# K/V preparation of the even layers, moved into the rest of their input projection

## The reference, cut to what matters

```python
def even_mixer(h, hc, w_in, ...):                 # w_in: 2048 x 5632
    k, v, q, bu, bv, ga, gb = split(h @ w_in, [512, 512, 1536, 512, 512, 1536, 512])
    q = apply_rope(rms_norm(heads(q, 12), q_g), cos, sin)
    k = apply_rope(rms_norm(heads(k, 4), k_g), cos, sin)    # per head of 128, then rotary
    attn = softmax(q k^T / sqrt(128)) v                     # 3 q heads share one k/v head
    sgu  = chunk_mlp(bu, bv, ...)
    out  = concat[attn * silu(ga), sgu * silu(gb)] @ w_out
```

## Time and profile before

| | us |
|---|---|
| median of 6 runs | 13523.53 |
| lowest, highest | 13475.0, 13628.33 |
| the profiled execution | 13583.81 |
| its span (core 1, the slowest) | 13582.2 |
| fastest core's span in it (core 4) | 13418.8 |

### The profile page before, as it was taken

How to read it: one execution, slowest core, us unless ns; L and a number is a source line. 1 busy time by engine, 2 the same in 40 slices (tenths; PEclk the granted TensorE clock), 3 DMA queues, 4 the chain that set the end, 5 groups by cost and what they waited for, 6 DMA issues and landing times.

```text
span 13582.2 us, 135689 instructions; the slowest of 8 cores (13418.8 to 13582.2 us)
## 1 busy us (share of the span) xinstructions
PE 6333.6 (47%) x36080; PEld 3450.9 (25%) x36080; DVE 4255.2 (31%) x6204; ACT 3173.7 (23%) x5611; POOL 2232.9 (16%) x1638
## 2 busy tenths in 40 slices
PE   2299155567691221021558953555849411211137
PEld 2144033343240111010223422333424211110014
DVE  0200432321212666416221023322121156652441
ACT  0200055530100222224111003555020012222330
POOL 0000322210002222222100022222000032223220
PEclk9599577777795555565667866777869755555558
DMA  7543110158432000111763321011953200002123
GB/s 113 184 108 107 59 34 30 37 93 188 120 90 60 11 11 11 56 52 40 132 181 103 100 67 40 32 34 35 186 161 93 87 9 11 11 13 85 38 55 102
DMA packets 649348, 1011.42 MB, mean 74 GB/s; under 512 B 112476, under 2 KB 523924, under 8 KB 590740
## 3 DMA queue, kind: packets, MB, share of 16 engines
q1 hardware_dynamic: 313144, 782.53, 17.3%
q0 software_dynamic: 335456, 220.22, 12.4%
HBM read 922.94 MB, written 299.89 MB: 90 GB/s over the span
## 4 chain that ended last, share of the span: by engine, by line
PE 40%; DVE 22%; DMA 12%; issue 10%; POOL 8%; ACT 7%; DVEq 1%; another core or an unknown queue 0%; POOLq 0%; SPq 0%; ACTq 0%
DVE PB L1104 3%; DMA ZY<-X 3%; PE gps_279 L433 1%; DVE lxc L1262 1%; PE gps_280 L433 1%; PE gps_282 L433 1%; PE gps_281 L433 1%; PE gps_48 L433 1%; PE gps_49 L433 1%; DMA adaw_18<-ada_w 1%; PE gps_50 L433 1%; PE gps_51 L433 1%; POOL htn L457 1%; DVE PB L1102 1%; POOL htb L466 1%
## 5 line engine op out<-in xcount | busy, mean ns | idle before, releaser
L1104 DVE TENSOR_TENSOR PB<-PB,X 128x576 f32<-128x576 f32 x224 | 425.2, 1898 | 23.0 <-DVE PB L1102 1.4
L593 ACT ACT_TABLE_LOAD x34 | 43.6, 1283 | 935.4 <-PE epS_313 L591 256.0
L451 POOL TENSOR_SCALAR hss<-hss 128x4 f32<-128x4 f32 (+1 forms) x72 | 14.3, 198 | 1161.5 <-DVE hss L449 1161.5
L1262 DVE SCALAR_TENSOR_TENSOR lxc<-lxd,lcw,lxc 128x255 f32<-128x255 f32 (+2 forms) x96 | 199.8, 2081 | 10.4 <-DVE lxc L1259 0.5
L572 PE MATMUL epT_311<-identb,rot 128*128 128x128 bf16 x144 | 21.1, 301 | 374.1 <-DVE rot L470 369.6
L572 PE MATMUL epT_80<-identb,rot 128*128 128x128 bf16 x144 | 21.1, 302 | 373.5 <-DVE rot L470 369.0
L649 PE MATMUL epG<-vnb,WST 128*128 128x128 bf16 x144 | 21.1, 301 | 360.4 <-POOL vnb L646 360.4
L1275 PE MATMUL lps_468<-lxcb,lwa_459 128*128 128x512 bf16 (+1 forms) x16 | 7.6, 478 | 372.2 <-ACT lxcb L1265 364.4
L1275 PE MATMUL lps_237<-lxcb,lwa_228 128*128 128x512 bf16 (+1 forms) x16 | 7.6, 478 | 372.0 <-ACT lxcb L1265 364.2
L433 PE MATMUL gps_279<-gw_273,AT 128*128 128x512 bf16 x480 | 127.3, 426 | 114.4 <-DMA gw_273<-ev_w_in 114.4
L642 POOL TENSOR_SCALAR hss<-hss 128x4 f32<-128x4 f32 x36 | 7.1, 197 | 980.7 <-DVE hss L640 980.7
(11 more groups left out here) (1259 smaller groups left out, 21248.6 us busy)
## 6 DMA issues: line engine op xcount, KB each, us to landing
nx_30<-xT SPq DMA_DIRECT2D x16, 1152.0 KB
nx_31<-xT SPq DMA_DIRECT2D x16, 1152.0 KB
uv<-ZE SPq DMA_DIRECT2D x36, 512.0 KB
nx_108<-xT SPq DMA_DIRECT2D x16, 1152.0 KB
nx_109<-xT SPq DMA_DIRECT2D x16, 1152.0 KB
ZO<-cst_122 SPq DMA_DIRECT2D x16, 1152.0 KB
ZO<-cst_123 SPq DMA_DIRECT2D x16, 1152.0 KB
ZY<-X SPq DMA_DIRECT2D x128, 144.0 KB
```

The costliest lines, as they stand in the source:

```text
L593: S.op("act", lambda e: e.activation(out=ESs[par][:, kt, 0:Q], in_=pss_[:, 0:Q], func=AF.Exp), reads=[bps_], writes=[bESs[par][kt]])
L1104: S.op("dve", lambda e: e.tensor_tensor(out=P_[:], in0=P_[:], in1=xin, op=ALU.add), reads=[bPq, bxin], writes=[bPq])
L1262: S.op("dve", lambda e, a0=a0, kk=kk, so=so, do=do, n_=n_, h=h: e.scalar_tensor_tensor(out=xc[:, a0 + do:a0 + do + n_], in0=xd[:, a0 + so: ...
```

## The change

`gemm_tok` now does the first two column blocks only (K and V). A new `gemm_tok_tail` for the other nine is recorded without being issued, inside `even_mixers`; its list of instructions is cut into seven equal pieces. Between the pieces stands the K/V preparation, now in six groups of three tiles: `kv_E` (loads, norm, rope) and `kv_P` (V loads, transposes, copies to `kT`). Where the cut falls takes no account of block borders. K and V no longer come in one load: K comes by SP, three loads of 256 KB per group into one buffer object, with six rope-table loads into one other (`CS3`); V comes straight into `VA` by POOL's queue, cast by the DMA, 18 loads in all. Norm and rope of K run on DVE alone except for the two small operations on POOL. In the tail ACT does all PSUM copies. Buffers that only attention needs are allocated after the tail, and the constants other than K's gain are loaded there. Two side edits: Q's rope tables have one buffer in place of two, and the gated MLP's product shares a scratch tile; in `s5_phase` the `SELC` copies go to DVE and the `SELR` copies to ACT.

```diff
-        def headnorm_rope(ph_bufs, src, nh, gtile, cos_t, sin_t, dst, eng2="pool"):
+        def headnorm_rope(ph_bufs, src, nh, gtile, cos_t, sin_t, dst, eng2="pool", ntile=1, cs_tstride=0):
...
+        def gemm_tok_tail(W, Z, n_list, stack):
...
+            for ni, n in enumerate(n_list):
+                w = wc[ni % 2]
+                S.dma("poolq", w[:], W[:, n * 512:(n + 1) * 512].rearrange("(kt p) n -> p kt n", p=128), writes=[bw[ni % 2]])
+                for t in range(NT):
...
+                    for kt in range(KT):
+                        S.op("pe", lambda e, j_=j_, w=w, kt=kt, t=t: e.matmul(
...
+                    S.op("act", lambda e, j_=j_: e.copy(out=st[j_][:], in_=pp[j_][:]), reads=[bpp[j_]], writes=[bst[j_]])
+                    S.dma("sp", Z[t * 128:(t + 1) * 128, n * 512:(n + 1) * 512], st[j_][:], reads=[bst[j_]], writes=[bz])
...
+                S.op("dve", lambda e: e.memset(VA[:], 1.0), writes=[bVA])
+
+                def kv_E(tg):
+                    r = raw[tg % 2]
+                    for i in range(3):
+                        t = tg * 3 + i
+                        S.dma("sp", r[:, i * 512:(i + 1) * 512], ZE[t * 128:(t + 1) * 128, 0:512], writes=[braw[tg % 2]])
+                        S.dma("sp", CS3[:, i, 0, :], rope_cos[t * 128:(t + 1) * 128, :], writes=[bCS3])
+                        S.dma("sp", CS3[:, i, 1, :], rope_sin[t * 128:(t + 1) * 128, :], writes=[bCS3])
...
+                    headnorm_rope(hb, r[:, 0:1536], 4, KG, CS3[:, 0, 0, :], CS3[:, 0, 1, :], rot[:, 0:12, :], ntile=3, cs_tstride=128, eng2="dve")
+
+                def kv_P(tg):
+                    for i in range(3):
+                        t = tg * 3 + i
+                        S.dma("poolq", VA[:, t, :, 0:128], ZE[t * 128:(t + 1) * 128, 512:1024].rearrange("p (h d) -> p h d", d=128), writes=[bVA])
+                        p = pT[i % 2]
+                        for h in range(4):
+                            S.op("pe", lambda e, p=p, h=h, i=i: e.transpose(out=p[:, h, :], in_=rot[:, i * 4 + h, :], identity=identb[:]), reads=[brot, bC], writes=[bpT[i % 2]])
+                        S.op("dve", lambda e, p=p, t=t: e.tensor_copy(out=kT[:, :, t * 128:(t + 1) * 128], in_=p[:]), reads=[bpT[i % 2]], writes=[bkT])
+
+                phg = ExitStack()
+                S.begin_capture()
+                gemm_tok_tail(ev_w_in[j], ZE, list(range(2, EVEN_IN // 512)), phg)
+                lg = S.end_capture()
+                NG_ = NT // 3
+                cut = [len(lg) * k // (NG_ + 1) for k in range(NG_ + 2)]
+                kv_E(0)
+                for tg in range(NG_):
+                    S.replay(lg[cut[tg]:cut[tg + 1]])
+                    kv_P(tg)
+                    if tg + 1 < NG_:
+                        kv_E(tg + 1)
+                S.replay(lg[cut[NG_]:])
+                S.barrier()
...
-                for t in range(NT):
-                    r = raw[t % 2]
-                    S.dma("sp", r[:, 0:1024], ZE[t * 128:(t + 1) * 128, 0:1024], writes=[braw[t % 2]])
...
-                    headnorm_rope(hb, r[:, 0:512], 4, KG, c_t, s_t, rot[:, 0:4, :])
...
-                            S.op("pool", lambda e, lo=lo, hi=hi, ri=ri, s_=s_, kc_=kc_: e.tensor_copy(out=SELC[lo:hi, ri, s_, :], in_=PN[lo:hi, ri, kc_, :]), reads=[bS], writes=[bS])
...
+                            S.op("dve", lambda e, lo=lo, hi=hi, ri=ri, s_=s_, kc_=kc_: e.tensor_copy(out=SELC[lo:hi, ri, s_, :], in_=PN[lo:hi, ri, kc_, :]), reads=[bS], writes=[bS])
+                            S.op("act", lambda e, lo=lo, hi=hi, ri=ri, s_=s_, kr_=kr_: e.copy(out=SELR[lo:hi, ri, s_, :], in_=PW[lo:hi, ri, kr_, :]), reads=[bS], writes=[bS])
...
-                    gemm_tok(l, ev_w_in[j], EVEN_IN, ZE)
+                    gemm_tok(l, ev_w_in[j], 1024, ZE)
```

More of the change, by code:

```diff
@@ L456, in headnorm_rope @@
             tn3 = tn[:, 0:W_].rearrange("p (h d) -> p h d", d=128)
[L457 to L462, removed]
@@ L463, in headnorm_rope @@
-            a3 = ta[:, 0:nh * 64].rearrange("p (h i) -> p h i", i=64)
-            b3 = tb_[:, 0:nh * 64].rearrange("p (h i) -> p h i", i=64)
+            S.op(eng2, lambda e: e.tensor_tensor(out=tn3, in0=tn3, in1=vw(gtile[:], [[0, H], [1, 128]]), op=ALU.mult), reads=[bscr, bC], writes=[bscr])
+            x0 = vw(tn[:, 0:1], [[nh * 128, ntile], [128, nh], [2, 64]], off=0)
+            x1 = vw(tn[:, 0:1], [[nh * 128, ntile], [128, nh], [2, 64]], off=1)
+            d0 = vw(dst, [[nh * 128, ntile], [128, nh], [2, 64]], off=0)
@@ L465, in headnorm_rope @@
+            d1 = vw(dst, [[nh * 128, ntile], [128, nh], [2, 64]], off=1)
+            cb = vw(cos_t, [[cs_tstride, ntile], [0, nh], [1, 64]])
+            sbb = vw(sin_t, [[cs_tstride, ntile], [0, nh], [1, 64]])
+            a3 = vw(ta[:, 0:1], [[nh * 64, ntile], [64, nh], [1, 64]])
+            b3 = vw(tb_[:, 0:1], [[nh * 64, ntile], [64, nh], [1, 64]])
             S.op("dve", lambda e: e.tensor_tensor(out=a3, in0=x0, in1=cb, op=ALU.mult), reads=[bscr, ph_bufs["bcs"]], writes=[ph_bufs["ba"]])
@@ L466, in headnorm_rope @@
             S.op(eng2, lambda e: e.tensor_tensor(out=b3, in0=x1, in1=sbb, op=ALU.mult), reads=[bscr, ph_bufs["bcs"]], writes=[ph_bufs["bb"]])
-            S.op("dve", lambda e: e.tensor_tensor(out=d4[:, :, :, 0], in0=a3, in1=b3, op=ALU.subtract), reads=[ph_bufs["ba"], ph_bufs["bb"]], writes=[bdst])
+            S.op("dve", lambda e: e.tensor_tensor(out=d0, in0=a3, in1=b3, op=ALU.subtract), reads=[ph_bufs["ba"], ph_bufs["bb"]], writes=[bdst])
             S.op("dve", lambda e: e.tensor_tensor(out=a3, in0=x0, in1=sbb, op=ALU.mult), reads=[bscr, ph_bufs["bcs"]], writes=[ph_bufs["ba"]])
@@ L469, in headnorm_rope @@
             S.op(eng2, lambda e: e.tensor_tensor(out=b3, in0=x1, in1=cb, op=ALU.mult), reads=[bscr, ph_bufs["bcs"]], writes=[ph_bufs["bb"]])
-            S.op("dve", lambda e: e.tensor_tensor(out=d4[:, :, :, 1], in0=a3, in1=b3, op=ALU.add), reads=[ph_bufs["ba"], ph_bufs["bb"]], writes=[bdst])
+            S.op("dve", lambda e: e.tensor_tensor(out=d1, in0=a3, in1=b3, op=ALU.add), reads=[ph_bufs["ba"], ph_bufs["bb"]], writes=[bdst])
+        def gemm_tok_tail(W, Z, n_list, stack):
+            AT = ATS["AT"]
+            wc = [sb(stack, "gtw%d" % i, [128, KT, 512], BF16) for i in range(2)]
+            st = [sb(stack, "gtst%d" % i, [128, 512], F32) for i in range(4)]
+            pp = [ps(stack, "gtps%d" % i, [128, 512]) for i in range(4)]
+            bw = [Buf(), Buf()]
+            bst = [Buf() for _ in range(4)]
+            bpp = [Buf() for _ in range(4)]
+            bz = Buf()
+            it = 0
+            for ni, n in enumerate(n_list):
+                w = wc[ni % 2]
+                S.dma("poolq", w[:], W[:, n * 512:(n + 1) * 512].rearrange("(kt p) n -> p kt n", p=128), writes=[bw[ni % 2]])
+                for t in range(NT):
+                    j_ = it % 4
+                    it += 1
+                    for kt in range(KT):
+                        S.op("pe", lambda e, j_=j_, w=w, kt=kt, t=t: e.matmul(
+                            pp[j_][:], lhsT=AT[:, kt, t * 128:(t + 1) * 128], rhs=w[:, kt, :], start=(kt == 0), stop=(kt == KT - 1)),
+                            reads=[bw[ni % 2], bAT[kt]], writes=[bpp[j_]])
+                    S.op("act", lambda e, j_=j_: e.copy(out=st[j_][:], in_=pp[j_][:]), reads=[bpp[j_]], writes=[bst[j_]])
+                    S.dma("sp", Z[t * 128:(t + 1) * 128, n * 512:(n + 1) * 512], st[j_][:], reads=[bst[j_]], writes=[bz])
@@ L474, in even_mixers @@
             with ExitStack() as ph:
-                CS = [sb(ph, "CS%d" % i, [128, 2, 64], F32) for i in range(2)]
-                bCS = [Buf(), Buf()]
+                CS = [sb(ph, "CS%d" % i, [128, 2, 64], F32) for i in range(1)]
+                bCS = [Buf()]
+                CS3 = sb(ph, "CS3", [128, 3, 2, 64], F32)
+                bCS3 = Buf()
                 KG = sb(ph, "KG", [128, 128], F32)
@@ L483, in even_mixers @@
                 VA = sb(ph, "VA", [128, NT, 4, 130], BF16)
[L484 to L488, removed]
                 raw = [sb(ph, "raw%d" % i, [128, 2048], F32) for i in range(2)]
-                uv = sb(ph, "uv", [128, 1024], F32)
                 sq = sb(ph, "hsq", [128, 1536], F32)
@@ L496, in even_mixers @@
                 rot = sb(ph, "rot", [128, 12, 128], BF16)
[L497 to L500, removed]
                 pT = [ps(ph, "epT%d" % i, [128, 4, 128], BF16) for i in range(2)]
[L502 to L505, removed]
                 braw = [Buf(), Buf()]
@@ new lines, in even_mixers @@
+                S.replay(lg[cut[NG_]:])
+                S.barrier()
+                phg.close()
+                qTs = [sb(ph, "qT%d" % i, [128, 12, 256], BF16) for i in range(2)]
+                bqTs = [Buf(), Buf()]
+                ESs = [sb(ph, "ES%d" % i, [128, NT, 256], BF16) for i in range(2)]
+                ATTs = [sb(ph, "ATT%d" % i, [128, 2, 1536], BF16) for i in range(2)]
+                bATTs = [Buf(), Buf()]
```

(11 more changed lines are left out.)

27 lines of the change are left out of this document (9 added, 18 removed).

## The result

| | us |
|---|---|
| median of the changed kernel, 8 runs | 13369.06 |
| lowest, highest | 13352.39, 13580.9 |
| kernel before, 16 runs | 13576.77 (13471.45 to 13730.58) |
| ratio, changed to before | 0.9896, 95% interval 0.9849 to 0.9943 |
| the profiled execution, and its span (core 5) | 13362.82, 13361.7 |

About 1% faster, 29 us above the forecast of 13340. In some executions of a kernel one die has a lower granted clock and is longer, as the die of cores 0 to 3 was in the profile of before (0.69 against 0.70), so the two profiles are compared on core 5, with a mean granted clock of 0.701 and 0.704: 13458.0 us before, 13361.7 after, 96 less.

What follows compares the result with a forecast made beforehand. PE bounds the even layers' projections; behind each, a 205 us K/V chain alternates between DVE and POOL. Net gains of 90.7 and 98.7 us, less 6 for S5 copies, take 183 off the median 13523.53: 13340, range 13235 to 13455.

Steps and rivals of the forecast that it cites:

- second cold start: At the tail's start, the first weight load stands behind group 0's power and SP's loads: 44.0 us per even layer.
- late weights: Tail weight loads behind a group's power land 37.5 us after its place; PE waits 41.5 us in layer 0, 33.5 in layer 2.
- Gain: Between the projection's last matmul and the first Q tile, 15.1 of 207.7 us stay: 192.6 gained per even layer.
- Table steps of 3.5: SP's rope-table loads share one buffer, each waiting for the one before: 3.5 us a step, three before the third K load.
- Slow tables: Rival, chance 0.14: table steps of 6.3 us under the projection's stores lengthen start and late loads, giving 13455.
- Slow groups: In the tail, the two long weight waits per layer each slow the next matmul group by 2.6 us: 5.2.
- DVE holds up the weight issue: Rival, chance 0.08: each tail load following a power waits 10 us till rope is done: +80, 13420.
- V loads choke POOL's queue: Rival, chance 0.06: 18 V loads wait in turn between weight loads; slower from v = 29 us each, 13745 at 35.
- SP's stores: In the tail, SP cannot store during five table waits, 17.5 us; buffers hold 27.6 us, so put at nothing.
- Q's single table buffer: In the Q loop, the one table buffer is refilled while the next tile is still squared; put at nothing.
- S5 copies: Selection copies spread over three engines: -3 to +16 us per layer, taken as +3, +6 in all.
- Clock: Rival, chance 0.08: a projection with pauses may keep its clock in layer 2, the 107 us: 13233.

Runs made afterwards that it cites:

- the first experiment: The changed kernel with each weight load of the projection's tail waiting once per semaphore, for the greatest value only; ratio 0.9798 to the kernel before.

## Why the prediction was right, and where it was wrong

The time came out in the range and the mechanism is the one told: the K/V loop went, and a second cold start and late weights took part of the gain back. One term was half its size, and that the time came so near is partly luck. On core 5 the gain was 96 us, not 183. But the forecast set out from a median that lay 65.5 us above core 5's span of before, while the changed kernel's median lies 7.4 above core 5's; this difference, which is no part of the sum, made up for 58 of the 87 us.

- *Gain, 192.6 less 11.2 for transposes, 181.4 per layer*: its 207.7 runs to the first Q tile's square at 1595.71, not to the first Q transpose as it says; the 20 us between stay in both kernels, so the gain isn't touched. The kernel with one list and loads ahead, where nothing else is left, has a stretch 186.4 shorter than before. Right within 5; a group's transposes cost about 1.4 us, not 1.9 (942.08 to 943.14 + 0.38).
- *Second cold start, 44.0*: 39.4 of wait and 2.4 in the slow group, 41.9 (38.3 in layer 2). Right in sum; without the barrier it is there as well, as the run with one list shows (49.7 of wait, walked waits in it).
- *Table steps of 3.5*: wrong one by one. SP's issues at the second group:

```profile
944.00 0.33 SPq L154 DMA_DIRECT2D CS_53<-rope_cos  x1
947.94 0.33 SPq L154 DMA_DIRECT2D CS_53<-rope_sin  x1
...
949.83 0.33 SPq L154 DMA_DIRECT2D CS_53<-rope_cos  x1
951.78 0.33 SPq L154 DMA_DIRECT2D CS_53<-rope_sin  x1
```

  The first takes 3.9, the next ones 1.9: three are 7.8, not 10.5. SP comes to them 1.2 us behind the cut and the third K load goes out at 952.20, 10.1 behind it, so the sum holds. Slow tables, the rival at 13455, fall with this.
- *Late weights: the path of 37.5 us* is the step that failed. The sign to look for was a load about 21 us behind PE's transposes; it came 35.9 behind. Measured at the first cut: power done 961.48 - 942.08 = 19.4 behind the transposes (20.9 forecast), **16.5 of walked waits (left out)**, and 995.91 - 977.98 = 17.9 until PE has the weights (16.6 forecast): 53.8. So 79.5 us of waits in place of 41.5, and 80.6 in place of 33.5, which also assumed layer 2's low clock of the earlier trace rows. Waits at four of the five cuts come near the sign named as wrong, waits at every block, but walked waits made them, not V loads. With the walk taken out the layer-0 waits are the forecast ones within 2.5 us each. The account had every operation and DMA ahead of the load on POOL, but took the wait itself as free once its event is past; the earlier trace rows couldn't show it, since there POOL waited 61 us in any case.
- *Slow groups, 5.2*: four of them, (6.36 + 6.00 + 5.62 + 4.98) - 4 x 3.62 = 8.5.
- *DVE holds up the weight issue* (0.08): it would have given a gap of 10 us. The gap was there and larger, but the first experiment removed it without touching DVE. The Trainium skill, "SBUF — State Buffer", section on the two separate sides, warns that DVE in a two-port mode keeps POOL from writing descriptors; for operations with two SBUF inputs it names only a POOL operation that reads SBUF. The traces agree with that clause: the issue at 969.08 took 1.23 us beside a DVE operation with two SBUF inputs, and the issues before the change 1.14. Whether a two-port operation would hold an issue up, no run here shows. The prediction says that no row of before has an issue beside such a DVE operation, but there are some. This one, in layer 1's RG-LRU part on core 5, lies inside three DVE operations in a row and takes 0.53 us; at 6031.68, with DVE idle, the same load's issue takes 0.54.

```profile
6125.03 7.26 DVE L1262 SCALAR_TENSOR_TENSOR lxc<-lxd,lcw,lxc 128x2047 f32<-128x2047 f32 x3
6128.21 0.53 POOL L154 DMA_DIRECT2D lwx_230<-lru_wx  x1 [5.66 <-DMA lwa_228<-lru_wa]
```

- *V loads choke POOL's queue*: v is 4.0 (873.25 to 877.21), as expected, far from the 29 where it would decide. The first V load of a group keeps POOL waiting for 14.5 to 28.7, but behind one or two weight loads, which the rival's sum counts already.
- *SP's stores*: blocked from 943.31 to 956.04, 12.7 us, not 17.5; PE never waited for a staging buffer there.
- *Q's single table buffer*, put at nothing: the stretch from first to last Q transpose is 6.4 and 3.6 us longer on core 5, and 3 to 4 of that go when the side edits are undone. The table buffer or the scratch tile costs a little; which one is open.
- *S5 copies, +3 per layer*: -3.3; the nearer end of the bounds was right.
- *Clock*: core 5 had its clock before and after, so whether pauses give it back stays open.

Of core 5's 96 us: -55.9 and -58.5 in the two stretches, +6.4 and +3.6 between first and last Q transpose, +8 elsewhere.

## What to carry to other kernels

A wait whose event is long past still takes its time on the queue that carries it. Where a scheduler notes one wait per reader, keep only the greatest value per semaphore, and count the waits ahead of a load as you count operations. When work is slipped between blocks, put the next block's load ahead of it on the issuing queue: that one move here was worth more than shortening the waits.

## What the runs showed of the hardware

A wait already satisfied costs POOL's queue about 57 ns (16.5 us for 289; 18.4 more for the 288 or so added, 64 ns each). It hides where the queue would be waiting anyway: the kernel before, with all its waits cut to the shortest, has the same stretches to 2 us and the same 0.65 us from a block's last matmul to the issue.

A DMA issue on POOL took 1.23 us beside a DVE operation of two f32 SBUF inputs and 1.14 without such a one, and for a smaller load 0.53 and 0.54: DVE held up none of those looked at.
